# Pairing an expert's FFN steps: 1024-column gate and up pieces, matmul terms in turn into two PSUM banks

## The reference, cut to what matters

```python
def moe_swiglu(h, w_router, b_router, w_gate, w_up, w_down):
    ...
    def expert_block(args):
        xb, e = args
        return (jax.nn.silu(xb @ w_gate[e]) * (xb @ w_up[e])) @ w_down[e]
```

## Time and profile before

| | |
|---|---|
| median of three runs | 1464.63 us (1464.58 to 1464.64) |
| span of the profiled execution | 1464.9 us |
| TensorE matmul busy | 1423.9 us, 97% |
| TensorE weight load busy | 1148.8 us, 78% |
| VectorE busy | 1139.5 us, 78% |
| ScalarE busy | 944.3 us, 64% |
| mean granted clock of TensorE | 0.989 |
| moved by DMA | 423.16 MB, mean 289 GB/s |

### The profile page before, as it was taken

The page is one execution under the profiler, slowest core; times in us unless marked ns, Lnnn a source line. Parts: engine busy times, 40 slices in busy tenths (PEclk is TensorE's granted clock), DMA queues, the critical chain, the costliest instruction groups (busy, mean ns, idle before and its releaser), DMA issues.

```text
span 1464.9 us, 17938 instructions
## 1 busy us (share of the span) xinstructions
PE 1423.9 (97%) x6483; PEld 1148.8 (78%) x6483; DVE 1139.5 (78%) x814; ACT 944.3 (64%) x773; POOL 20.5 (1%) x26
## 2 busy tenths in 40 slices
PE   6999999999989999999999999999999999999995
PEld 5888888787867887887788788778878878887884
DVE  4454666655568889888888988888898888888887
ACT  5354334444657767777776777777777777777775
POOL 0000000000120000000000000000000000000001
PEclk9999999999989999999999999999999999999998
DMA  9258775552149998998999899899989989999991
GB/s 358 97 172 217 200 216 173 167 197 96 50 132 337 358 367 304 360 360 318 357 361 368 305 370 369 298 361 356 361 314 362 380 303 350 365 349 337 367 365 76
DMA packets 192979, 423.16 MB, mean 289 GB/s; under 512 B 19184, under 2 KB 21360, under 8 KB 192944
## 3 DMA queue, kind: packets, MB, share of 16 engines
q1 hardware_dynamic: 179728, 418.15, 79.7%
q10 hardware_dynamic: 12784, 3.26, 1.6%
q0 software_dynamic: 432, 1.28, 0.3%
HBM read 421.61 MB, written 1.05 MB: 289 GB/s over the span
## 4 chain that ended last, share of the span: by engine, by line
PE 92%; DVE 3%; ACT 2%; issue 2%; POOL 0%; DMA 0%; ACTq 0%; DVEq 0%; POOLq 0%
PE bank_G L992 10%; PE bank_G L994 10%; PE bank_G L993 10%; PE bank_U L992 9%; PE bank_U L994 9%; PE bank_U L993 9%; PE bank_Y L992 8%; PE bank_Y L994 8%; PE bank_Y L993 8%; PE bank_T L1330 2%; DVE w_lo L621 1%; PE bank_T L992 1%; PE bank_G L1227 1%; PE bank_T L993 1%; PE bank_T L994 1%
## 5 line engine op out<-in xcount | busy, mean ns | idle before, releaser
L621 DVE TENSOR_TENSOR w_lo<-raw,w_hi 128x2048 fp32r<-128x2048 f32 x394 | 898.2, 2290 | 227.1 <-ACT w_hi L362 226.1
L362 ACT ACTIVATE w_hi<-raw 128x2048 fp32r<-128x2048 f32 x394 | 754.5, 1917 | 308.4 <-PE bank_U L994 99.8
L992 PE MATMUL bank_Y<-w_hi,hidT_hi 128*128 128x512 f32 x492 | 195.3, 397 | 0.0
L994 PE MATMUL bank_Y<-w_hi,hidT_lo 128*128 128x512 f32 x492 | 194.6, 395 | 0.0
L993 PE MATMUL bank_Y<-w_lo,hidT_hi 128*128 128x512 f32 x492 | 194.5, 395 | 0.0
L992 PE MATMUL bank_U<-w_hi,xg_hi 128*128 128x512 f32 x448 | 182.1, 406 | 0.2
L992 PE MATMUL bank_G<-w_hi,xg_hi 128*128 128x512 f32 x448 | 178.7, 399 | 0.9 <-DVE w_lo L621 0.4
L994 PE MATMUL bank_G<-w_hi,xg_lo 128*128 128x512 f32 x448 | 177.7, 397 | 0.0
L993 PE MATMUL bank_G<-w_lo,xg_hi 128*128 128x512 f32 x448 | 177.6, 396 | 0.0
L993 PE MATMUL bank_U<-w_lo,xg_hi 128*128 128x512 f32 x448 | 176.9, 395 | 0.0
L994 PE MATMUL bank_U<-w_hi,xg_lo 128*128 128x512 f32 x448 | 176.8, 395 | 0.0
(11 more groups left out here) (262 smaller groups left out, 1489.2 us busy)
## 6 DMA issues: line engine op xcount, KB each, us to landing
raw<-in_expert_w_gate SPq DMA_DIRECT2D x114, 1024.0 KB, 6.5
raw<-in_expert_w_up SPq DMA_DIRECT2D x113, 1024.0 KB, 6.7
raw<-in_expert_w_down SPq DMA_DIRECT2D x112, 1024.0 KB, 6.4
raw<-in_nat_w_qkv SPq DMA_DIRECT2D x12, 1024.0 KB, 5.0
raw<-in_ffn_w_gate SPq DMA_DIRECT2D x11, 1024.0 KB, 7.8
raw<-in_ffn_w_up SPq DMA_DIRECT2D x11, 1024.0 KB, 5.4
raw<-in_ffn_w_down SPq DMA_DIRECT2D x11, 1024.0 KB, 5.3
raw<-in_fourier_w_in SPq DMA_DIRECT2D x4, 1024.0 KB, 11.5
```

Source lines behind the costliest of these rows:

```text
L362: nc.scalar.activation(w_hi[w][:], raw[s][:], ACT.Copy).then_inc(hi_made, 1)
L621: nc.vector.tensor_tensor(w_lo[w][:], raw[s][:], w_hi[w][:].bitcast(f32), ALU.subtract).then_inc(lo_made, 1)
L992: nc.tensor.matmul(out_, xh, wh, start=start, stop=False)
L994: return nc.tensor.matmul(out_, xl, wh, start=False, stop=stop)
```

## The change

The seven steps become groups: step 0 alone, then steps (1, 2), (3, 4), (5, 6). In a pair the pieces of w_gate and w_up hold 2 row tiles by 1024 columns, both steps at once; there are eight of gate, eight of up and four of down in a group. The number of pieces (42), their size and the rings stay. The order is gate g, up g, down g-1. TensorE works a piece off with the new `both`, which issues each of the three terms for both banks before the next term: for gate and up into G[1] and G[0] (U[1] and U[0]) at once, for down into Y[0] and Y[1]. The expert's last down piece keeps `three`. ScalarE and VectorE run their small steps for both members of a group one after the other. The gathered tokens now go to `X = [G[0], G[1]]` in place of G[1] and U[1], and the work around the end of the expert is laid out anew. In the diff, parts that only rename or follow from this are left out.

```diff
+GROUPS = [(0,)] + [(c, c + 1) for c in range(1, STEPS, 2)]
+LAST = len(GROUPS) - 1
+assert GROUPS[-1][-1] == STEPS - 1
+
+
+def piece_parts(g):
+    return range(2 * len(GROUPS[g]))
+
+
 def expert_pieces():
 
     order = []
-    for c in range(STEPS):
-        order += [("gate", c, 0), ("gate", c, 1), ("up", c, 0), ("up", c, 1)]
-        if c:
-            order += [("down", c - 1, 0), ("down", c - 1, 1)]
-    order += [("down", STEPS - 1, 0), ("down", STEPS - 1, 1)]
+    for g in range(len(GROUPS)):
+        order += [(kind, g, part) for kind in ("gate", "up") for part in piece_parts(g)]
+        if g:
+            order += [("down", g - 1, part) for part in piece_parts(g - 1)]
+    order += [("down", LAST, part) for part in piece_parts(LAST)]
     return order, {x: j for j, x in enumerate(order)}
+
+
+def group_end(kind, g):
+    return (kind, g, piece_parts(g)[-1])
+
+
+def down_place(c, half):
+
+    g = (c + 1) // 2
+    return ("down", g, 2 * GROUPS[g].index(c) + half)
...
-    kind, c, half = EXPERT[j]
+    kind, g, part = EXPERT[j]
+    c0, width = GROUPS[g][0], BANK * len(GROUPS[g])
     v = {"gate": ewg, "up": ewu, "down": ewd}[kind][0].rearrange("e (k p) n -> p (e k) n", p=P)
     if kind == "down":
-        return v[:, bass.ds(e * (FFE // P) + (BANK // P * c + KROW * half), KROW), :], KROW, D
-    return v[:, bass.ds(e * KD + KH * half, KH), BANK * c:BANK * (c + 1)], KH, BANK
+        return v[:, bass.ds(e * (FFE // P) + (BANK // P * c0 + KROW * part), KROW), :], KROW, D
+    tiles = PIECE // width
+    return v[:, bass.ds(e * KD + tiles * part, tiles), BANK * c0:BANK * c0 + width], tiles, width
...
+    X = [G[0], G[1]]
...
         def silu(E, c):
-            act.wait_ge(piece_used, piece(AT["gate", c, 1], E))
+            act.wait_ge(piece_used, piece(AT[group_end("gate", (c + 1) // 2)], E))
...
-            for j, (kind, c, half) in enumerate(EXPERT):
-                if (kind, half) == ("gate", 1):
-                    silu(E, c)
-                    if c:
-                        hidden_hi(E, c - 1)
-                if (kind, c, half) == ("up", STEPS - 1, 1):
+            for j, (kind, g, part) in enumerate(EXPERT):
+                if (kind, g, part) == group_end("gate", g):
+                    for c in GROUPS[g]:
+                        silu(E, c)
+                    for c in GROUPS[g - 1] if g else ():
+                        hidden_hi(E, c)
+                if (kind, g, part) == group_end("up", LAST):
                     gather_copy(E + (sweep + 2))
-                if (kind, c, half) == ("down", STEPS - 2, 0):
+                if (kind, g, part) == ("down", LAST - 1, 1):
                     gather_hi(E + (sweep + 2))
+                    hidden_hi(E, STEPS - 2)
+                if (kind, g, part) == ("down", LAST - 1, 3):
                     hidden_hi(E, STEPS - 1)
-                if (kind, c, half) == ("down", STEPS - 1, 1):
+                if (kind, g, part) == group_end("down", LAST):
                     result_hi(E)
                 split_hi(j + SPLIT, E)
...
+                if (kind, g, part) == group_end("gate", 0):
                     next_selection(E, e, sweep)
-                elif (kind, half) == ("gate", 1):
-                    hidden_rest(E, c - 1)
-                if (kind, half) == ("up", 1):
-                    hidden(E, c)
-                    if c == STEPS - 1:
+                elif (kind, g, part) == group_end("gate", g):
+                    for c in GROUPS[g - 1]:
+                        hidden_rest(E, c)
+                if (kind, g, part) == group_end("up", g):
+                    for c in GROUPS[g]:
+                        hidden(E, c)
+                    if g == LAST:
                         gather_copy(E + (sweep + 2))
-                if (kind, c, half) == ("down", STEPS - 2, 0):
+                if (kind, g, part) == ("down", LAST - 1, 1):
                     gather_lo(E + (sweep + 2))
+                    hidden_rest(E, STEPS - 2)
+                if (kind, g, part) == ("down", LAST - 1, 3):
                     hidden_rest(E, STEPS - 1)
...
+        def both(outs, xh, xl, whs, wls, start, stop):
+
+            for out_, wh in zip(outs, whs):
+                nc.tensor.matmul(out_, xh, wh, start=start, stop=False)
+            for out_, wl in zip(outs, wls):
+                nc.tensor.matmul(out_, xh, wl, start=False, stop=False)
+            for out_, wh in zip(outs, whs):
+                last = nc.tensor.matmul(out_, xl, wh, start=False, stop=stop)
+            return last
...
-            def columns(kind, c, bk):
-                for half in range(2):
-                    j = AT[kind, c, half]
+            def columns(kind, g, banks):
+                tiles = PIECE // (BANK * len(GROUPS[g]))
+                outs = [banks[c % 2][:] for c in GROUPS[g]]
+                cols = [slice(BANK * i, BANK * (i + 1)) for i in range(len(outs))]
+                for part in piece_parts(g):
+                    j = AT[kind, g, part]
                     ready(j, E)
-                    if (kind, c) == ("gate", 0):
-                        pe.wait_ge(e_xlo, 2 * (E + sweep) + half + 1)
-                    wh, wl = parts(j, E, KH)
-                    for k in range(KH):
-                        kk = KH * half + k
-                        last = three(bk[:], mo["xg_hi"][:, kk], mo["xg_lo"][:, kk], wh[:, k], wl[:, k], kk == 0, kk == KD - 1)
+                    wh, wl = parts(j, E, tiles)
+                    for k in range(tiles):
+                        kk = tiles * part + k
+                        if (kind, g) == ("gate", 0) and kk % 4 == 0:
+                            pe.wait_ge(e_xlo, 2 * (E + sweep) + kk // 4 + 1)
+                        last = both(outs, mo["xg_hi"][:, kk], mo["xg_lo"][:, kk], [wh[:, k, cs] for cs in cols],
+                                    [wl[:, k, cs] for cs in cols], kk == 0, kk == KD - 1)
                     last.then_inc(piece_used, 1)
...
-                order = [(k, q) for k in range(KROW) for q in range(2)]
-                if (c, half) == (STEPS - 1, 1):
-                    order.sort(key=lambda kq: kq[1])
-                for k, q in order:
-                    kk = KROW * half + k
-                    cs = slice(BANK * q, BANK * (q + 1))
-                    last = three(Y[q][:], hidT_hi[c % 2][:, P * kk:P * (kk + 1)], hidT_lo[c % 2][:, P * kk:P * (kk + 1)],
-                                 wh[:, k, cs], wl[:, k, cs], c == 0 and kk == 0, c == STEPS - 1 and kk == BANK // P - 1)
-                    if (c, half, k, q) == (STEPS - 1, 1, KROW - 1, 0):
-                        last.then_inc(e_y, 1)
+                halves = [slice(BANK * q, BANK * (q + 1)) for q in range(2)]
+                if (c, half) != (STEPS - 1, 1):
+                    for k in range(KROW):
+                        kk = KROW * half + k
+                        last = both([bk[:] for bk in Y], hidT_hi[c % 2][:, P * kk:P * (kk + 1)], hidT_lo[c % 2][:, P * kk:P * (kk + 1)],
+                                    [wh[:, k, cs] for cs in halves], [wl[:, k, cs] for cs in halves], c == 0 and kk == 0, False)
+                else:
+                    for q in range(2):
+                        for k in range(KROW):
+                            kk = KROW * half + k
+                            last = three(Y[q][:], hidT_hi[c % 2][:, P * kk:P * (kk + 1)], hidT_lo[c % 2][:, P * kk:P * (kk + 1)],
+                                         wh[:, k, halves[q]], wl[:, k, halves[q]], False, k == KROW - 1)
+                        if q == 0:
+                            last.then_inc(e_y, 1)
...
-            for c in range(STEPS):
-                if c == 0:
+            for g, group in enumerate(GROUPS):
+                if g == 0:
                     pe.wait_ge(e_silu, E * STEPS)
-                elif c == 1:
+                else:
+                    pe.wait_ge(e_silu, E * STEPS + (group[-1] - 1))
+                if g == 1:
                     pe.wait_ge(e_added, E)
-                else:
-                    pe.wait_ge(e_silu, E * STEPS + (c - 1))
-                columns("gate", c, G[c % 2])
-                if c == 0:
+                columns("gate", g, G)
+                if g == 0:
                     pe.wait_ge(e_added, E)
                     pe.wait_ge(e_sel, E + (sweep + 1))
                     for b in range(NB):
                         last = nc.tensor.transpose(T[1][:, P * b:P * (b + 1)], mo["sel"][:, b].bitcast(f32), ident[:])
                     last.then_inc(e_selT, 1)
                 else:
-                    hidden_transposes(c - 1)
-                if c != 1:
-                    pe.wait_ge(e_hid, E * STEPS + max(c - 1, 0))
-                columns("up", c, U[c % 2])
-                if 1 <= c < STEPS - 1:
-                    down(c - 1, 0)
-                    down(c - 1, 1)
+                    for c in GROUPS[g - 1]:
+                        hidden_transposes(c)
+                pe.wait_ge(e_hid, E * STEPS + max(group[-1] - 1, 0))
```

(54 more changed lines are left out.)

4 lines of the change are left out of this document (2 added, 2 removed).

## The result

The changed kernel takes 1468.37 us (median of 10 runs, 1466.47 to 1469.85), the kernel before 1465.06 us (10 runs, 1464.27 to 1466.31). The ratio is 1.002, with a 95% interval of 1.0011 to 1.0028: 3.3 us slower, on the edge of what this measurement can tell. The forecast was 1465.8 us, no measurable change.

The account below looks back on a forecast made before the run. TensorE's own instruction stream was taken as the bound. Span 1464.9 us plus 1.2 for late pieces, loads and matmul order at 0, gave 1466.1, as a median 1465.8 us; own range 1463 to 1467.5, over all 1444.5 to 1470.5 us.

Parts of the forecast that it names:

- the four signs: 24 starts in 5.60 us; expert 0.15 us longer; w_hi at T+2.4 (T: last gate matmul's start); up's third-piece load 0.2 late.
- TensorE's stream is the bound: In each expert, TensorE's 504 matmuls at 0.2333 us between starts take 117.6 of the 127 us.
- The loads cost nothing: Gate and up loads of steps 1 to 6 get 4 KB rows, keeping number and size; costed at nothing.
- The order of the matmuls is worth 0: Alternating banks and repeated stationary in 3552 gate, up and down matmuls: taken as 0, bounds 0 and 24.5 us gain.
- Rival 1: Alternating banks shortens matmul spacing: 24.5 us gained, 5.3 us lost to late pieces, 1445.4 us; chance 0.28.
- the prediction's estimate of 60 us: On TensorE, a saved stationary load would be worth some 60 us by the skill page; outside sum and range.
- The pairing makes three pieces per expert late: After gate of groups 1 to 3, doubled small steps delay w_lo: 0.15 us lost per expert, 1.2 us in eight.
- The late pieces behind two `hidden` and at the end of the expert cost nothing: w_lo at up's end is done at T+17.7, just when asked; at expert's end 13.9 against 14.5; no cost.
- Rival 2: ScalarE's small steps after gate cost 0.60 us each, not 0.48: 0.72 us per expert, 5.8 us, 1470.4 us; chance 0.25.
- The median 0.3 us under the span: Whole kernel: the median of the runs lies 0.3 us under the profiled span, turning 1466.1 into 1465.8 us.

Follow-up runs that it names:

- e3: The changed kernel with one more 128x512 ACTIVATE (a copy from bank G) between silu and hidden_hi of groups 1 to 3; 1480.95 us.
- e7: The changed kernel with gate and up of groups 1 to 3 streaming hn_hi and hn_lo in place of the weights; 1457.44 us, one run.
- e1: The changed kernel with each term triple finished in one bank before the other's, wide pieces and pairing kept; 1469.18 us.
- e4: The kernel before with only down's terms alternating between the Y banks in 13 of 14 down pieces per expert; 1464.74 us.
- e2: The changed kernel with w_hi and w_lo made ahead of the small steps at the gate end of groups 1 to 3; 1464.88 us.

## Why the prediction was right, and where its sum was off

The mechanism held, its size didn't. 1468.37 us lies in the range over all (1444.5 to 1470.5 us) but 0.9 us above the forecast's own range (1463 to 1467.5 us), and +3.3 us is a little over the 2.9 us that the prediction called no change. By `e3` another 0.1 us in the same chain would have cost 24 x 0.1 = 2.4 us more; that the result stayed near the limit is in part luck. Of the four signs, two came as forecast (the spacing, and `w_hi` at T+2.4); the load was 0.29 us late, not 0.2, and the expert 0.36 us longer, not 0.15.

- **TensorE's stream is the bound**: held. The largest changes of the time, -7.3 us (`e7`) and +15.4 us (`e3`) against the kernel before, are TensorE's spacing and its wait for `w_lo`.
- **The loads cost nothing**: held. 25% fewer packets (192979 on the page of before, 143827 after) changed nothing, and no engine waits for a load of an expert's weights.
- **The order of the matmuls is worth 0**: held, and shown three ways: spacing of 0.2333 us after, `e1` and `e4` alone. The objection to it, the gather's 0.227 us, was rightly set aside as "one of operands or state": it follows the moving operand (`e7`). Rival 1 (1445.4 us) fell with `e1` and `e4`. The Trainium skill (TensorE: Matmul & The Clock Gate, "Step-by-step: what each phase is for") lets many matmuls use one load; `both` lines up four with one stationary, each still has its load (6483 of both), and no run shows a saving, so nothing here bears out the prediction's estimate of 60 us for one.
- **The pairing makes three pieces per expert late**: the mechanism, its place and its count held; `e2` takes it away and `e3` enlarges it. Its size is the term that was off. Predicted: `w_hi` at T+2.38, `w_lo` done at T+6.62, load at T+6.68 against T+6.49, late by 0.19, lost 0.06 us. Measured in groups 2 and 3: T+2.43, T+6.70, T+6.75 against T+6.46 (738.70 to the due start at 745.16), late by 0.29, lost 0.17 us. Group 1 came as predicted, 0.02 us lost for 0.03. 0.05 us came from a first `silu` at T+0.51 where the earlier trace rows had 0.44, 0.02 to 0.03 from `w_lo` behind `w_hi` (1.98 us, not 1.95), 0.03 from the transposes, eight of which take less than twice four. About 0.12 us of lateness was absorbed, as predicted (0.13). Since only the excess over 0.13 us counts, an error of 0.1 us in a chain of 6.7 nearly tripled the loss. Per expert 0.36 us was lost, not 0.15: 2.9 us, not 1.2.
- **The late pieces behind two `hidden` and at the end of the expert cost nothing**: held; no row of `w_lo` has more than the 24 new waits.
- **Rival 2** was the same mechanism at full size, and the result lies between the two: 0.36 us per expert, where the forecast had 0.15 and the rival 0.72. Its sign came in part: of the three new waits per expert two take 0.33 us, over its 0.2, the third 0.20. Its threshold, 0.12 us per group (24 x 0.12 = 2.9 us), was just reached, 0.36 / 3 = 0.12. So the total time doesn't part the forecast from the rival; what does is the rival's premise, the small steps at 0.60 us each, which didn't hold: the pitch was 0.48 to 0.49 us, in `e3` too.
- **The median 0.3 us under the span**: a run here takes 1.7 to 1.9 us more than its own span (1467.57 against 1465.8 after), so the execution profiled before must have been longer than the three timed; its own time isn't known. This did no harm, since 1465.8 us is the three-run median plus 1.2. The forecast time was 2.6 us too low: 2.1 us by the term above (1.2 against 3.3), and 0.4 us because ten runs of the kernel before have 1465.06 us where the three had 1464.63.

## What to carry to other kernels

Where a pipeline of splits or casts has a fixed number of buffers, put the step that refills a buffer ahead of the small steps that became possible at the same moment: that took 0.3 us per expert off the kernel before, at the one place where a piece was late, and 0.7 us in the changed kernel. Doubling the small steps at one point, even with the same total, used up the margin at that point: cost such a change there, to 0.1 us, and treat a margin below the reading error as gone. A different order of accumulation banks gained nothing here; look at the starts of matmuls that already have it, and at what else sets them apart.

## What was not expected of the hardware

A matmul of 512 fp32r columns starts every 0.2333 us when its moving operand is `w_hi`, `w_lo`, `act_hi` or `act_lo`, and every 0.2267 us in a long run with `hn_hi` and `hn_lo` (`e7`), with the same stationary, banks and granted clock (1.00 in the stages of both). Bank order, stationary operand, place in the partition, start modulo 64 and rewriting by other engines were each changed alone, and none of them is the cause by itself; the cause is not found. The estimate of 27 us is what it would be worth at most: `e7`, with 288 of the 504 matmuls of an expert, got 1.23 us per expert, 9.9 us in eight, in a single run.
